# A two-layer encoder trunk on one core: the transposed x comes from the host instead of from TensorE, and x itself is asked for later

## What is computed

```python
for l in range(DEPTH):                       # DEPTH = 2
    h = rms_norm(x, norm_g[l])               # x * rsqrt(mean(x*x)) * g
    p = h @ w_in[l]                          # 2048 x about 13,000 columns
    p_sb, p_mla, p_rw, p_gate = split_cols(p, (SB_COLS, MLA_COLS, RW_COLS, GATE_COLS))
    ...
    rw_main = rw_main + rw_mu[l] * (prev - rw_main)     # prev: the token before
    ...
    x = x + merged @ w_out[l]
```

## Time and profile before

| what | value |
|---|---|
| median of 3 runs | 1691.61 us (1690.33 to 1692.40) |
| the profiled execution's own time | 1692.25 us |
| its span, first to last instruction | 1690.5 us |
| TensorE busy | 99% of the span |
| VectorE, ScalarE, GpSimd busy | 67%, 49%, 29% |
| moved from and to HBM | 194 GB/s over the span |

### The profile page before, as it was taken

The page is one execution under the profiler, slowest core; times in us unless marked ns, Lnnn a source line. Parts: engine busy times, 40 slices in busy tenths (PEclk is TensorE's granted clock), DMA queues, the critical chain, the costliest instruction groups (busy, mean ns, idle before and its releaser), DMA issues.

```text
span 1690.5 us, 22088 instructions
## 1 busy us (share of the span) xinstructions
PE 1677.6 (99%) x8394; PEld 1399.2 (83%) x8394; DVE 1134.9 (67%) x1579; ACT 836.6 (49%) x1181; POOL 487.8 (29%) x722
## 2 busy tenths in 40 slices
PE   8999999999999999999999999999999999999999
PEld 7878888888888888888888788888888888888887
DVE  5668575766976566886656775756669666578853
ACT  6454453435544455554454454434445554555532
POOL 1011212410343426362410112233203534244500
PEclk9999999999999999999999999999999999999999
DMA  8865655655666557785687555556556565668754
GB/s 277 243 193 182 175 177 170 184 165 173 178 184 176 173 164 234 236 302 188 205 269 226 176 186 172 187 152 188 174 167 178 167 178 177 192 212 279 267 193 157
DMA packets 176913, 332.82 MB, mean 197 GB/s; under 512 B 19516, under 2 KB 32746, under 8 KB 176808
## 3 DMA queue, kind: packets, MB, share of 16 engines
q1 hardware_dynamic: 167048, 297.86, 57.7%
q0 software_dynamic: 9584, 33.48, 5.7%
q10 hardware_dynamic: 176, 0.07, 0.0%
HBM read 311.20 MB, written 16.78 MB: 194 GB/s over the span
## 4 chain that ended last, share of the span: by engine, by line
PE 92%; DVE 3%; ACT 2%; DMA 2%; issue 1%; SPq 1%; ACTq 0%; DVEq 0%
PE D L707 83%; PE B L707 8%; DMA ring<-in_w_in 2%; DVE w_lo L1398 1%; ACT w_hi L1026 1%; DVE xy L1398 0%; ACT arena L1026 0%; ACT gev L1026 0%; PE B L898 0%; DVE arena L1398 0%; DVE gev L1444 0%; PE B L877 0%; SPq L435 0%; ACT L1026 0%; DVE arena L1428 0%
## 5 line engine op out<-in xcount | busy, mean ns | idle before, releaser
L1398 DVE TENSOR_TENSOR w_lo<-ring,w_hi 128x1024 fp32r<-128x1024 f32 (+3 forms) x560 | 675.7, 1219 | 342.1 <-ACT w_hi L1026 334.0
L1026 ACT ACTIVATE w_hi<-ring 128x1024 fp32r<-128x1024 f32 (+3 forms) x560 | 575.0, 1038 | 463.9 <-PE D L707 361.5
L707 PE MATMUL D<-w_hi,ht_hi 128*128 128x512 f32 (+2 forms) x1728 | 681.3, 394 | 3.0 <-DVE w_lo L1398 2.8
L707 PE MATMUL D<-w_hi,ht_lo 128*128 128x512 f32 (+2 forms) x1728 | 666.0, 385 | 0.0
L707 PE MATMUL D<-w_lo,ht_hi 128*128 128x512 f32 (+2 forms) x1728 | 665.1, 385 | 0.0
L707 PEld LDWEIGHTS D<-w_hi,ht_hi 128*128 128x128 f32 x1728 | 325.1, 188 | 71.4 <-issue 7.8
L707 PEld LDWEIGHTS D<-w_hi,ht_lo 128*128 128x128 f32 x1728 | 324.5, 188 | 65.3
L707 PEld LDWEIGHTS D<-w_lo,ht_hi 128*128 128x128 f32 x1728 | 325.2, 188 | 59.0 <-issue 0.5
L609 POOL COPY arena<-arena 32x256 f32<-32x256 f32 x240 | 163.1, 680 | 144.7 <-DVE arena L1428 109.3
L707 PEld LDWEIGHTS B<-arena 128*66 128x66 f32 (+3 forms) x1312 | 134.2, 165 | 24.3 <-issue 8.2
L707 PE MATMUL B<-arena 128*66 128x64 f32 (+7 forms) x1312 | 144.7, 263 | 0.6 <-ACT arena L1026 0.6
(11 more groups left out here) (160 smaller groups left out, 1376.9 us busy)
## 6 DMA issues: line engine op xcount, KB each, us to landing
ring<-in_w_in SPq DMA_DIRECT2D x368, 512.0 KB, 4.5
ring<-in_w_out SPq DMA_DIRECT2D x64, 512.0 KB, 5.2
ring<-in_w_br_mla SPq DMA_DIRECT2D x32, 512.0 KB, 5.2
gate_spill<-gev POOLq DMA_DIRECT2D x24, 512.0 KB, 4.7
arena<-gate_spill POOLq DMA_DIRECT2D x24, 512.0 KB, 5.2
ring<-in_mla_w_ukv SPq DMA_DIRECT2D x16, 512.0 KB, 4.0
ring<-in_w_br_rw SPq DMA_DIRECT2D x16, 512.0 KB, 5.2
ring<-in_w_br_sb SPq DMA_DIRECT2D x16, 512.0 KB, 5.2
```

The source lines that it names most:

```text
L707: return nc.tensor.matmul(o, a, b, start=start, stop=stop, skip_group_check=True)
L1026: return nc.scalar.activation(o, i, fn, **kw)
L1398: return v.tensor_tensor(o, a, b, op)
```

## The change

The host also lays x out by features (`xt`, four blocks of 512 KB, each 128 partitions by four blocks of 256 tokens) and the gains as columns. The first layer's operand is made from these, without TensorE. SyncE asks for `xt` where it asked for x, and for the quarters of x after chunks 8 to 11. ScalarE squares x two pieces at a time behind the high halves of chunks 12 to 15, and only then makes `rs` and takes `wk` out. `AT_LORA` becomes 17. The rows that were asked for before chunk 12 are asked for before chunk 20, the constants after the shift of `rk`. Three pairs of semaphores become one each, with the counts carried on over the layers.

```diff
-AT_LORA = END["wk"] + 8
+AT_LORA = END["wk"] + 9
...
+        XT = [arena[:, j * 1024:(j + 1) * 1024] for j in range(3)] + [arena[:, at_mkv:at_mkv + 1024]]
...
             for j in range(4):
-                first_x(j)
+                sp.dma_start(XT[j], xt[j].rearrange("p (k t) -> p k t", k=4)).then_inc(xt_in[j], 16)
                 if j < LEAD:
                     first_chunk(j)
...
+                    if l == 0 and 2 * RING < n <= 3 * RING:
+                        first_x(n - 2 * RING - 1)
...
-                    if n == 3 * RING:
+                    if n == 5 * RING:
                         row(GR[:, 0:QK], mla_qn_g[l], rows_in[l])
...
-                            cells_in = [(cqg, mla_q_norm_g[l]), (ckg, mla_kv_norm_g[l])]
-                            if following < DEPTH:
-                                cells_in += [(ng, norm_g[following])]
-                            for dst, src in cells_in:
+                            for dst, src in ((cqg, mla_q_norm_g[l]), (ckg, mla_kv_norm_g[l])):
                                 sp.dma_start(dst, columns(src)).then_inc(small_in[l], 16)
+                        if following < DEPTH:
+                            sp.dma_start(ng, gain_cols[following]).then_inc(small_in[l], 16)
...
-                if l == 0:
-                    pool.wait_ge(split_lo, END["wk"] + 2)
-                    pool.dma_start(con[:, P:K_END], consts[:, P:K_END]).then_inc(con_in, 16)
                 for i in range(3):
                     pool.wait_ge(dense_ev[l], GI["rr"] + i + 1)
                     shift(PV[:, :, i * 512:(i + 1) * 512], R[:, :, i * 512:(i + 1) * 512], r_shift[i][l])
+                    if l == 0 and i == 1:
+                        pool.dma_start(con[:, P:K_END], consts[:, P:K_END]).then_inc(con_in, 16)
...
-            pe.wait_ge(id_in, 16)
             for l in range(DEPTH):
                 at[0] = beats[0] = 0
                 if l == 0:
-                    pe.wait_ge(gain_rows, 16)
-                    mm(D[3][:, 0:KD], NG16, ident[0:KD, 0:KD], True, True).then_inc(gain_columns, 1)
-                    for j in range(4):
-                        pe.wait_ge(x_moved[j], 16)
-                        if j >= 2:
-                            pe.wait_ge(first_xl, 2 * j - 2)
-                        transposes((2 * j, 2 * j + 1), j * 512, first_pe)
-                        if j:
-                            dense_to(2 * j)
+                    dense_to(END["wk"])
+                    pe.wait_ge(id_in, 16)
...
+            act.dma_start(ng, gain_cols[0]).then_inc(first_gain, 16)
             act.dma_start(con[:, 0:P], consts[:, 0:P]).then_inc(id_in, 16)
-            act.dma_start(NG16, norm_g[0].rearrange("(k p) -> k p", p=P)).then_inc(gain_rows, 16)
...
+            def first_columns_hi(c):
+                act.wait_ge(xt_in[c // 2], 16)
+                for k in (2 * c, 2 * c + 1):
+                    last = f(hth[:, k, :], XT[k // 4][:, k % 4, :], scale=ng[:, k:k + 1])
+                last.then_inc(first_xh, 1)
...
-                    first_split(0)
-                    columns_hi(0, first_pe, first_xh)
-                    ...
-                    dense_to(7)
-                    first_squares(7)
-                    at[0] = END["wk"]
-                    split(END["wk"] + LEAD - 1)
+                    for c in range(KD // KC):
+                        first_columns_hi(c)
+                        if c < LEAD:
+                            first_split(c)
+                        else:
+                            dense_to(c + 1 - LEAD)
+                    dense_to(END["wk"] - 1)
+                    while at[0] < END["wk"] + 5:
+                        at[0] += 1
+                        split(at[0] + LEAD - 1)
+                        if at[0] > END["wk"] + 1:
+                            first_squares(2 * (at[0] - END["wk"]) - 4, 2 * (at[0] - END["wk"]) - 3)
...
+            def first_columns_lo(c):
+                dve.wait_ge(first_xh, c + 1)
+                for k in (2 * c, 2 * c + 1):
+                    last = v.scalar_tensor_tensor(htl[:, k, :], XT[k // 4][:, k % 4, :], ng[:, k:k + 1],
+                                                  hth[:, k, :].bitcast(F32), ALU.mult, ALU.subtract)
+                last.then_inc(first_xl, 1)
...
-                    first_split(0)
-                    columns_lo(0, first_xh, first_xl)
-                    ...
-                    dense_to(7)
+                    for c in range(KD // KC):
+                        first_columns_lo(c)
+                        if c < LEAD:
+                            first_split(c)
+                        else:
+                            dense_to(c + 1 - LEAD)
+                    dense_to(END["wk"] + 5)
                     sum_squares(first_sq, first_sum, 8)
```

More of the change, by code:

```diff
@@ L197, in program @@
             rw_mu, rw_w0, rw_w_up, rw_a0, rw_a_up, rw_k_k, rw_k_a, rw_r_k, rw_gn_g, rw_gn_b,
-            w_br_sb, w_br_mla, w_br_rw, w_out, consts, out, spill):
+            w_br_sb, w_br_mla, w_br_rw, w_out, consts, xt, gain_cols, out, spill):
     weights = dict(w_in=w_in, uq=mla_w_uq, ukv=mla_w_ukv, bs=w_br_sb, bm=w_br_mla, br=w_br_rw, w_out=w_out)
@@ L296, in program @@
         at_mkv = used[0]
+        XT = [arena[:, j * 1024:(j + 1) * 1024] for j in range(3)] + [arena[:, at_mkv:at_mkv + 1024]]
+        XT = [t.rearrange("p (k t) -> p k t", k=4) for t in XT]
         MKV = take(2048).rearrange("p (b h n c) -> p b h n c", b=2, h=2, n=2)
@@ L304, in program @@
         GR = take(2 * QK)
-        NG16 = GR[0:KD, 0:P]
         used[0] = 2 * KD * SEQ
@@ L374, in program @@
         x_in, x_new = [one(f"x_back{j}") for j in range(4)], sem("x_new")
-        blocks_turned, rows_moved = sem("blocks_turned"), sem("rows_moved")
-        quadrants = sem("quadrants_moved")
+        blocks_turned, rows_moved = one("blocks_turned"), one("rows_moved")
+        quadrants = one("quadrants_moved")
         x_settled = sem("x_settled")
@@ L386, in program @@
         first_gain, first_hi, first_lo = (one("first_" + n) for n in ("gains", "weights_hi", "weights_lo"))
-        gain_rows, gain_columns = one("gain_rows_in"), one("gain_columns")
+        xt_in = [one(f"columns_of_x_in{j}") for j in range(4)]
         first_pe, first_xh, first_xl, first_sq, first_sum = (s[-1] for s in (xt_pe, xt_act, xt_dve, x_sq, x_sum))
@@ L602, in move @@
                     if parts[0] == 0:
-                        pool.wait_ge(blocks_turned[l], q + 1)
+                        pool.wait_ge(blocks_turned, 9 * l + q + 1)
                     turned = TURN[q >= 3].rearrange("p (h k j t) -> p h k j t", h=2, k=4, j=4)
@@ L609, in move @@
                             nc.gpsimd.tensor_copy(moved[32 * j:32 * j + 32, :, :, i, :],
-                                                  turned[32 * i:32 * i + 32, :, :, j, :]).then_inc(quadrants[l], 1)
-                        pool.wait_ge(quadrants[l], 16 * q + 4 * d + 4)
+                                                  turned[32 * i:32 * i + 32, :, :, j, :]).then_inc(quadrants, 1)
+                        pool.wait_ge(quadrants, 144 * l + 16 * q + 4 * d + 4)
                     if parts[-1] == 3:
-                        pool.sem_inc(rows_moved[l], 1)
+                        pool.sem_inc(rows_moved, 1)
                 beat(GN_BEATS)
@@ L1230, in renewed_hi @@
             def renewed_hi(j):
-                act.wait_ge(rows_moved[l], 7 + j)
+                act.wait_ge(rows_moved, 9 * l + 7 + j)
                 for s in (2 * j, 2 * j + 1):
@@ L1244, in squares @@
                 act.wait_ge(done, j + 1)
+            act.dma_start(ng, gain_cols[0]).then_inc(first_gain, 16)
             act.dma_start(con[:, 0:P], consts[:, 0:P]).then_inc(id_in, 16)
-            act.dma_start(NG16, norm_g[0].rearrange("(k p) -> k p", p=P)).then_inc(gain_rows, 16)
             act.wait_ge(once, 3)
             act.preload_act_table_set("natural_log_exp_and_others")
-            act.wait_ge(gain_columns, 1)
-            f(ng, D[3][:, 0:KD]).then_inc(first_gain, 1)
-            act.wait_ge(first_gain, 1)
+            act.wait_ge(first_gain, 16)
             def first_split(n):
@@ L1349, in branch_hi @@
                 def branch_hi(q, t, k0):
-                    act.wait_ge(rows_moved[l], q + 1)
+                    act.wait_ge(rows_moved, 9 * l + q + 1)
                     for i in range(2):
@@ L1366, in _ @@
                     dense_to(merged_at(j))
-                    act.wait_ge(rows_moved[l], 4 + j)
+                    act.wait_ge(rows_moved, 9 * l + 4 + j)
                     for s in range(2):
@@ L1424, in turn_blocks @@
                 if q:
-                    dve.wait_ge(rows_moved[l], q)
+                    dve.wait_ge(rows_moved, 9 * l + q)
                 if q == 1:
                     dve.wait_ge(sb_moved, 2 * l + 2)
-                v.transpose(TURN[q >= 3].rearrange("p (h c) -> p h c", h=2), block).then_inc(blocks_turned[l], 1)
```

(11 more changed lines are left out.)

21 lines of the change are left out of this document (removed).

## The result

| | before | after |
|---|---|---|
| median of 6 runs each, us | 1691.77 | 1698.95 |
| lowest and highest, us | 1690.33, 1692.40 | 1696.97, 1701.08 |
| profiled execution, us | 1692.25 | 1698.74 |
| its span, us | 1690.5 | 1697.0 |

The ratio is 1.0045, with an interval of 1.0034 to 1.0057: slower by 7.2 us, of which 6.5 show between the two profiled executions.

What follows compares the result with a forecast made beforehand. TensorE, busy 99% of the span, was taken as the bound, with time lost where it has nothing ready. Chunk 17 at 57.9 less 50.6, less 0.5, gave 6.8 us slower: 1698.4 us, range 1690.5 to 1702.5.

Steps and rivals of the forecast that it cites:

- Step 1: Start of the kernel: with `xt` landing at 5.3, TensorE's first product comes at 7.7 us, against 9.37 before.
- the rival of the clock: TensorE's clock falls to 1.2 GHz in the wait before chunk 17, costing 1.6 us: 1700 to 1701.6; chance 0.15.
- Step 2: Chunks 0 to 7: VectorE sets the pace at 1.54 us a chunk, chunk 8 starts at 22.6, 2.0 us won.
- Step 3: Transfers between chunks 8 and 12: 2.1 MB of x added, chunk 12 lands at 36.0 and starts at 38.4.
- Step 4: Chain behind the late squares: last square at 45.8, then clears, shift and mixing; TensorE gets on to chunk 17 at 57.9.
- Behind chunk 17: Rows, constants and gains asked for later: nothing in the first layer, 0.5 us won before the second layer's chunk 12.
- The kept lead: Rival: chunk 12 lands before 31.5 and TensorE goes on without a gap; faster, 1688.2 us; chance 0.07.
- The short wait: Rival: fast transfers and a quick shift put chunk 17 at 53.1, +2.0 us, 1693.6; chance 0.25.
- `xt` did land like x: Answers a rival at the start: if `xt` landed later than x, 2.0 us more are lost; no chance given.

## Why the prediction was right

The time (1698.4 against 1698.95), the sign and the mechanism of the forecast held. Some of its terms were off, and that they made up for each other to within 0.6 us is luck:

| step | predicted | measured |
|---|---|---|
| 1, first product | 7.7 | 8.11 |
| 2, chunk 8 starts | 22.6 | 23.66 |
| 3, chunk 12 lands / starts | 36.0 / 38.4 | 35.4 / 37.96 |
| 4, last square done | 45.8 | 45.2 |
| 4, landing of the shift | 5.5 | 4.65 |
| 4, chunk 17 starts | 57.9 | 56.37 |
| rival, cost of the clock | not in the sum | 1.6 |
| 5, all behind chunk 17 | -0.5 | -0.8 |

**Step 1** was 0.4 early, and its sum followed the wrong operand. `xt` landed 3.9 us after its request (4.5 taken), and the columns were ready at 6.84; but chunk 0 landed only at 6.61, and its two halves, 0.63 and 0.69, set the start at 8.11. The first two chunks then ran at the lower pace, 2.70 for chunk 0 against 1.52 before, as the rival of the clock had said (2.9). **Step 2** named the wrong bound: VectorE's low half of chunk 7 was done at 20.3, even before the 21.1 reckoned, but chunk 8 had landed only at 21.2, 5.04 after its request at 16.14. I had taken the date from VectorE's pace and hadn't added the landing to the request. The halves then took 1.06 and 1.23 us, and TensorE waited 1.42.

**Step 3** put the landing 0.6 too late. The transfers of `x` had been given 6.2 us; run alone they showed 5.8 at chunk 12. The rows, given 1.8, were worth 2.2 when they were put back. The engines moved 386 to 402 GB/s from 25 to 35 us, above the 339 I had used; at 390, an estimate, 2.1 MB take 5.4 us instead of 6.2. These are of the size of the 0.6; what each gave was not separated.

**Step 4** held link for link: four times 2.46 us of ScalarE from the landing (35.42 to 45.2 are 9.8), 0.1 to the clears, 4.5 (predicted 4.74) to the third DMA, then the landing and 1.34. Only the shift's landing was 0.85 short of my value, inside its bounds of 4.2 to 6. As to such landings the Trainium skill (DMA: Bandwidth & Descriptors, Anatomy of one DMA — SWDGE (gpsimd) path) states a fixed cost of about 2.0 us; this trace has 4.65 for the 0.5 KB of the shift's third DMA, with the engines 0.86 busy from 50 to 55 us, so here the measurement decides, and a landing of 2.0 would have been 2.65 too short.

Chunk 17 was thus 1.5 early. **The rival of the clock** came true beside the forecast, not in its place: 1.6 us, the size I had put on it, and it nearly filled the 1.5. The granted clock of 0.50 from 58 to 60 us is the lower of the two levels, 1.2 GHz, after TensorE had stood idle for 3.38 us, with 0.61 some 3 us before. The Trainium skill (TensorE: Matmul & The Clock Gate, Part 1: The HAM clock gate) states that the throttled clock is the default and activity releases it; this trace agrees. My inference that the longer wait is the likelier to bring it is not borne out: 2.23 us brought it in one kernel, and 3.38 did not in another. So the 1.6 is the price of a fall that may or may not come, and the sum should have carried it with a chance: the earlier trace rows showed the half pace already at the start, and I left it out because the column of the earlier trace rows read 1.00 there. It reads 1.00 in the changed kernel's first products too, which stand 0.21 apart until 12.7 us and 0.12 apart after, so at the start of a run the spacing is to be believed.

**Behind chunk 17**: 1692.25 - 50.72 = 1641.5 us before, 1642.4 after; less the clock's 1.6, it is 0.8 better (0.5 predicted). Two executions can't tell these 0.3 apart.

**The other rivals.** The kept lead needed chunk 12 by 31.5; it landed at 35.4, and even without x the mixing was 1.46 late. The short wait needed a chunk 17 at 53.1. `xt` did land like x (3.9 us after its request, x 4.5).

Together: the order costs 4.6 us alone, the transfers 7.3 alone, and the early start and the moved rows give back 2.6 together (the kernel without x). 4.6 + 7.3 - 2.6 = 9.3. The clock's 1.4 to 1.6 stands in each of the first two, and in the changed kernel's trace it is paid once, which leaves about 7.8 against the measured 7.2. The transfers may partly run in time won at the start; the remainder of 0.6 was not separated.

## What to carry to other kernels

Before a load is moved behind others, follow its last user in order, not its first: here the squares had 3 us of room through five links (take-out, clears, shift, mixing, transposes), and were put off by 19. Bytes added to a stretch in which the DMA engines are full cost nearly their whole transfer time (5.8 of 6.2 us), and a wait of TensorE of some 3 us (2.74 to 3.38) cost half as much again in clock in four of the five that were traced, so it belongs in the sum with a chance. And if data is laid out a second way, ask whether the first is still needed: dropping x from the start turned a loss of 7.2 us into a gain of 2.9.

## What the runs showed of the hardware

- A reduction of 1024 columns to 256 over a strided view took 2.02 us on VectorE; two additions that do the same took 1.15 (up to 1.69 beside GpSimd's work).
- Float32 products of 128 by 128 with the identity took 0.22 us each, two instructions; float32 transposes of the same size at the full clock stand about 0.1 apart. Idle work put into a wait has to be sized by its own row.
- The 512 KB load of chunk 8 took 5.04 us to land in the changed kernel (16.14 to 21.18), with the DMA engines 0.78 busy over that time.
- The clock fell after waits of 3.38, of 2.74 with 0.64 before, of 3.25, and, in the kernel with the rows put back, after one of 2.23 at chunk 11 and one of 3.14 before the transposes. It did not after 2.14 in the changed kernel at chunk 11, nor after 2.55 and 2.65 there in the two with the idle products, nor after 3.38 in the kernel with the large row moved. So a wait's length alone doesn't decide it; what does stays open. A fall took 1.4 to 1.8 us of TensorE's pace, and none of the time where TensorE had to wait for its next chunk anyway (the rows put back).
